# Five reorderings in a single-core two-block kernel: first unit by passes, taps, convolution, additions, weight halves

## What is computed

```python
# first block
hn = rmsnorm(h, norm1_g); proj = hn @ w_in
u, q, k, v, g_ssm, g_att = split(proj)
y_ssm = s5_mixer(u, ...)            # diagonal complex state space, scanned, then a gated unit
o = diff_attention(q, k, v, ...)    # 4 heads, two softmaxes each, causal, ALiBi
mixed = sigmoid(g_ssm) * (y_ssm @ w_ssm_out) + sigmoid(g_att) * (y_att @ w_att_out)
h = h + mixed @ w_o
h = h + conv_glu_ffn(rmsnorm(h, norm2_g), w_up, conv_w, conv_b, w_down)
# second block
z = rms_norm(x, norm_mix) @ w_in
a_x, a_y, b_q, b_f, b_i, b_g, c_q, c_k, c_v = split(z)
ya = rglru_group(a_x, a_y, ...)     # convolution of 4 taps, gates, a scan
yb = hgrn2_group(b_q, b_f, b_i, b_g, ...)
yc = moba_group(c_q, c_k, c_v)      # 8 heads, causal
x = x + concat(rms_norm(ya), yb, rms_norm(yc)) @ w_out
x = x + square(relu(rms_norm(x, norm_mlp) @ w_ff1)) @ w_ff2
out = rms_norm(x, norm_final)
```

## Time and profile before

| | |
|---|---|
| median of 3 runs | 721.42 us (719.54 to 721.86) |
| the profiled execution's own time | 720.89 us |
| its span, first to last instruction | 719.2 us |
| TensorE busy | 702.1 us, 98% of the span |
| VectorE, ScalarE, GpSimd busy | 75%, 54%, 4% |
| mean granted TensorE clock | 0.996 |
| chain that ended last, by engine | PE 80%, DVE 13%, ACT 4%, issue 3% |

### The profile page before, as it was taken

How to read it: one execution, slowest core, us unless ns; L and a number is a source line. 1 busy time by engine, 2 the same in 40 slices (tenths; PEclk the granted TensorE clock), 3 DMA queues, 4 the chain that set the end, 5 groups by cost and what they waited for, 6 DMA issues and landing times.

```text
span 719.2 us, 14645 instructions
## 1 busy us (share of the span) xinstructions
PE 702.1 (98%) x6172; PEld 664.1 (92%) x6172; DVE 536.1 (75%) x953; ACT 390.4 (54%) x600; POOL 26.0 (4%) x50
## 2 busy tenths in 40 slices
PE   7999998999999999999999999999999999999997
PEld 6999997888999999999999989889999899998995
DVE  6899899557978877777678899965877655655653
ACT  7586557368366454444445874498653444434433
POOL 3001000000000000000000340000000000000000
PEclk9999999999999999999999999999999999999999
DMA  8752343233555555555555553333355556655541
GB/s 248 218 167 61 95 147 112 62 111 125 179 173 180 195 193 194 177 176 181 189 198 193 186 167 127 118 118 118 118 190 185 182 176 193 200 191 177 187 165 59
DMA packets 94701, 115.68 MB, mean 161 GB/s; under 512 B 7971, under 2 KB 83932, under 8 KB 94636
## 3 DMA queue, kind: packets, MB, share of 16 engines
q1 hardware_dynamic: 94244, 114.51, 48.8%
q0 software_dynamic: 128, 0.13, 0.1%
q10 hardware_dynamic: 264, 0.10, 0.1%
HBM read 113.69 MB, written 1.05 MB: 160 GB/s over the span
## 4 chain that ended last, share of the span: by engine, by line
PE 80%; DVE 13%; ACT 4%; issue 3%; POOL 0%; DVEq 0%; POOLq 0%; ACTq 0%
PE psum L1842 16%; PE psum L1843 16%; PE psum L1844 16%; PE psum L2440 4%; PE psum L2438 4%; PE psum L2439 4%; DVE w_lo L1101 3%; PE psum L2196 3%; PE psum L2200 3%; PE psum L2198 3%; ACT w_hi L500 1%; PE psum L1989 1%; PE psum L2024 1%; PE psum L1934 1%; DVE sz L1020 1%
## 5 line engine op out<-in xcount | busy, mean ns | idle before, releaser
L1101 DVE TENSOR_TENSOR w_lo<-w_raw,w_hi 128x2048 fp32r<-128x2048 f32 x105 | 239.4, 2289 | 70.1 <-ACT w_hi L500 69.9
L500 ACT ACTIVATE w_hi<-w_raw 128x2048 fp32r<-128x2048 f32 x105 | 199.0, 1906 | 57.2 <-PE psum L2440 28.2
L1842 PE MATMUL psum<-x2n_hi,w_hi 128*128 128x256 f32 x400 | 114.3, 286 | 1.7 <-DVE w_lo L1101 0.7
L1843 PE MATMUL psum<-x2n_lo,w_hi 128*128 128x256 f32 x400 | 112.0, 280 | 0.0
L1844 PE MATMUL psum<-x2n_hi,w_lo 128*128 128x256 f32 x400 | 112.0, 280 | 0.0
L1842 PE MATMUL psum<-hs_hi,w_hi 128*128 128x256 f32 (+1 forms) x352 | 99.6, 283 | 0.0
L1843 PE MATMUL psum<-hs_lo,w_hi 128*128 128x256 f32 (+1 forms) x352 | 99.2, 282 | 0.0
L1844 PE MATMUL psum<-hs_hi,w_lo 128*128 128x256 f32 (+1 forms) x352 | 98.9, 281 | 0.0
L1842 PEld LDWEIGHTS psum<-x2n_hi,w_hi 128*128 128x128 f32 x400 | 75.2, 188 | 4.9 <-DVE x2n_lo L1562 1.0
L1844 PEld LDWEIGHTS psum<-x2n_hi,w_lo 128*128 128x128 f32 x400 | 76.2, 191 | 0.0
L1843 PEld LDWEIGHTS psum<-x2n_lo,w_hi 128*128 128x128 f32 x400 | 75.2, 188 | 0.6
(11 more groups left out here) (461 smaller groups left out, 1535.0 us busy)
## 6 DMA issues: line engine op xcount, KB each, us to landing
w_raw<-in_w_ff_dram SPq DMA_DIRECT2D x32, 1024.0 KB, 5.2
w_raw<-in_w_in_dram SPq DMA_DIRECT2D x27, 1024.0 KB, 5.3
w_raw<-in_w_up_dram SPq DMA_DIRECT2D x22, 1024.0 KB, 5.1
w_raw<-in_w_down_dram SPq DMA_DIRECT2D x11, 1024.0 KB, 5.0
w_raw<-in_w_o_dram SPq DMA_DIRECT2D x4, 1024.0 KB, 5.1
w_raw<-in_w_out_dram SPq DMA_DIRECT2D x4, 1024.0 KB, 5.4
w_raw<-in_w_ssm_out_dram SPq DMA_DIRECT2D x2, 1024.0 KB, 5.1
w_raw<-in_w_att_out_dram SPq DMA_DIRECT2D x2, 1024.0 KB, 5.1
```

What stands on the lines that cost most here:

```text
L500: A.activation(w_hi[:, u % NW, :], raw[:, u % NRAW, :], ACT.Copy).then_inc(sem("hi_ready"), 1)
L1101: V.tensor_tensor(w_lo[:, u % NRAW, :], raw[:, u % NRAW, :], w_hi[:, u % NW, :].bitcast(F32), ALU.subtract).then_inc(sem("lo_ready"), 1)
L1842: T.matmul(out_, lh, rh, start=start, stop=False)
L1843: T.matmul(out_, lh, rl, start=False, stop=False)
```

## The change

In the first unit the loops over passes and groups change places: each pass is done for both groups before the next. On ScalarE `split_to(14)` and the tanh of gate unit 3 move behind the output's copy, the exponentials and the taps' copies; on VectorE `split_to(14)` moves behind the second half's scan, mix and back-rotation. In the second block one `scale` of `hgq` moves ahead of the small columns, `lru_conv(1)` moves behind level 5 and `m_norm(1)`, and `m_max(1)` ahead of a weight half. At the output unit the scaling of `mo` comes ahead of `hgg`, all four of its low halves behind the reciprocal, and each weight half behind both of a unit's additions instead of between the first addition and its low half. Nothing is added or removed; the numbers of instructions of each kind stay the same.

```diff
--- before.py
+++ after.py
@@ -719,12 +719,12 @@
             copy_b(0)
             outputs_by_phase()
             gates(2)
-            split_to(14)
-            gates(3)
             copy_o(0)
             exp_b(1)
             copy_a(1)
             taps()
+            gates(3)
+            split_to(14)
             split_to(15)
             exp_a(2)
             gates(4)
@@ -1671,6 +1671,7 @@
             for m in range(2):
                 scale("hg_f", 0, m, hgf[:, m, :])
             two_after("hg_f")
+            scale("hg_q", 0, 0, hgq[:, 0, :])
             dve.wait_ge(sem("tiny_a"), 3)
             seq(V.tensor_scalar(sm("sp_m", 2), lam, -1.0, 0.0, ALU.mult, ALU.max))
             seq(tt(sm("sp_m", 2), sm("sp_m", 2), sm("sp_l", 2), ALU.add))
@@ -1685,8 +1686,7 @@
                 seq(V.tensor_scalar(hgf[:, m, :], hgf[:, m, :], sm("lb_c", 2)[:, m:m + 1], sm("lb_m", 2)[:, m:m + 1],
                                     ALU.mult, ALU.add))
                 seq(V.tensor_scalar(hgk[:, m, :], hgk[:, m, :], sm("lb_c", 2)[:, m:m + 1], None, ALU.mult))
-            for m in range(2):
-                scale("hg_q", 0, m, hgq[:, m, :])
+            scale("hg_q", 0, 1, hgq[:, 1, :])
             two_after("hg_q")
             dve.wait_ge(sem("w2_act"), 6)
             tt(hqf[:, :, :], hgq[:, :, :], hgf[:, :, :], ALU.mult).then_inc(sem("h_level"), 1)
@@ -1706,15 +1706,15 @@
             scale("lru_x", 0, 1, lru_g[:, 1, :])
             level(3)
             two_after("lru_x")
-            lru_conv(1)
             scale("cq", 1, 0, cq[:, 2, :], 0.125)
             level(4)
             scale("cq", 1, 1, cq[:, 3, :], 0.125)
+            m_max(1)
             two_after("cq", 1)
-            m_max(1)
             scale("ck", 1, 0, ck[:, 2, :])
             level(5)
             m_norm(1)
+            lru_conv(1)
             two_after("ck", 1)
             scale("ck", 1, 1, ck[:, 3, :])
             level(6)
@@ -1750,7 +1750,6 @@
             V.reciprocal(sm("hg_root", 8), sm("hg_root", 8)).then_inc(sem("hg_r"), 1)
             dve.wait_ge(sem("yc_rms"), 1)
             seq(V.reciprocal(rst3[:, :], rst3[:, :]))
-            scale("hg_g", 0, 0, hgg[:, 0, :])
 
             def y_low(n_, kt, src):
                 dve.wait_ge(sem("ycat_hi"), n_ + 1)
@@ -1759,11 +1758,10 @@
             for p_ in range(4):
                 STT(out=mo[:, p_, :], in0=mo[:, p_, :], scalar=col("att_norm", p_), in1=rst3[:, :],
                     op0=ALU.mult, op1=ALU.mult).then_inc(sem("yc"), 1)
-            for p_ in range(2):
-                y_low(p_, 4 + p_, mo[:, p_, :])
+            scale("hg_g", 0, 0, hgg[:, 0, :])
             dve.wait_ge(sem("ya_rms"), 1)
             mark(V.reciprocal(rst2[:, :], rst2[:, :]))
-            for p_ in range(2, 4):
+            for p_ in range(4):
                 y_low(p_, 4 + p_, mo[:, p_, :])
             dve.wait_ge(sem("dve_seq"), n[0])
             for m in range(2):
@@ -1794,10 +1792,9 @@
                     tt(x2[:, 2 * i + m, :], x2[:, 2 * i + m, :], banks[g % NB][:, 0:256], ALU.add).then_inc(
                         sem(f"group_free{g % NB}"), 1)
                     x3_square(2 * i + m - 1)
-                    if m == 0:
-                        split_to(unit_at[("w_out2", i)]["n"] + 3 - i // 3)
                     taken(dve, g)
                     x_low("x3", "norm_mlp", 2 * i + m)
+                split_to(unit_at[("w_out2", i)]["n"] + 3 - i // 3)
             x3_square(7)
             split_to(unit_at[("ff1", 0)]["n"] + 2)
             dve.wait_ge(sem("norm_root"), 2)
@@ -1924,8 +1921,8 @@
             def first_unit():
                 wh, wl = (w[:, 0, :].rearrange("p (k n) -> p k n", k=KD) for w in (w_hi, w_lo))
                 for h in range(2):
-                    for m in range(2):
-                        for n_, (w, x) in enumerate(((wh, xn_hi), (wh, xn_lo), (wl, xn_hi))):
+                    for n_, (w, x) in enumerate(((wh, xn_hi), (wh, xn_lo), (wl, xn_hi))):
+                        for m in range(2):
                             if m == 0 and n_ != 1:
                                 pe.wait_ge(sem((("first_hi", "hi_ready")[h], "", ("first_lo", "lo_ready")[h])[n_]), 1)
                             for kt in range(4 * h, 4 * h + 4):
@@ -1933,8 +1930,8 @@
                                     pe.wait_ge(sem(("xn_hi", "xn_lo")[n_]), kt + 1)
                                 last = T.matmul(banks[m][:, 0:TOK], w[:, kt, P * m:P * m + P], x[:, kt, :],
                                                 start=(kt == 0 and n_ == 0), stop=(kt == KD - 1 and n_ == 2))
-                        if h == 1:
-                            last.then_inc(sem("group_done"), 1)
+                            if h == 1 and n_ == 2:
+                                last.then_inc(sem("group_done"), 1)
 
             def second_unit():
                 wh, wl = w_hi[:, 1, :].rearrange("p (k n) -> p k n", k=KD), w_lo[:, 1, :].rearrange("p (k n) -> p k n", k=KD)
```

## The result

The changed kernel takes 713.63 us (median of six executions, 711.83 to 715.46); the kernel before took 720.48 us beside it (six, 717.79 to 721.86). The profiled execution of the changed kernel took 714.82 us (span 713.1) against 720.89 (span 719.2).

A forecast was written before the change was run, and what follows sets the result against it. TensorE is busy nearly throughout; seven rows of its waits hold 7.0 us. Terms 1.0 + 2.4 + 0.0 + 1.0 + 0.6 + 0.8 = 5.8 us off 720.89 give 715.1, forecast as 715.5 us, range 713.9 to 718.4.

The forecast's parts named there:

- Rival 3: Whole kernel: the gain is a loan, transfers or a full engine set the pace; 719.3 to 721.4 us, chance 9%.
- First unit: Group 1's 8 matmuls run ahead of the wait for w_lo; 1.0 us won if the slow clock stretch stays.
- The ceiling: First unit's gain at unit 3 is at most 1.7 us, since VectorE's w_lo ends at 31.67 us at the earliest.
- Rival 1: The clock holds in the first unit: 0.7 us more won there, 714.8 us, chance 20%.
- Rival 5: Alternating PSUM banks in the first unit loses the clock: 3 us lost, 718.5 us, chance 2%.
- Taps: Attention output's copy on ScalarE starts at 115.05 instead of 117.45 us, ahead of a weight half: 2.4 us won.
- hgq: Scaling ahead of the small columns removes a 0.4 us wait, which moves on to hqf: 0.0 us.
- Convolution: lru_conv(1) behind level 5 removes TensorE's 0.9 us wait for that level's copy, plus the restart: 1.0 us won.
- Output unit: mo's additions first win 0.6 us; weight halves behind both rounds win 0.8 us.
- Rival 2: A close margin of four fails: one miss gives back 0.7 us, several up to 2.5; 716.2 to 718.0 us, chance 24%.
- the other three margins: Slack of 0.3 to 0.5 us at the output unit's half, level 5's copy and m_norm(1).
- Rival 4: Output unit's halves come late if a round takes 2.6 us or more, not 1.46; at 3 us, 724.8 us; chance 3%.

The follow-up runs named there:

- e15: The kernel before, unedited, one more profiled execution: 718.33 us.
- e12: The changed kernel, unedited, run a third time: median 713.24 us, ratio to the kernel before 0.9874.
- e4: The changed kernel with the weight half and gate unit 3's tanh back ahead of the attention output's copy: 718.94 us.
- e2: The changed kernel with the scaling of hgq back behind the small columns: 714.81 us.
- e5: The changed kernel with lru_conv(1) and m_max(1) back where they stood before: 714.07 us.
- e6: The changed kernel with hgg's scaling ahead of the output unit's four additions again and the low halves in two pairs: 715.47 us.
- e7: The changed kernel with each weight half of the output unit back between the first addition and its low half: 715.32 us.
- e1: The changed kernel, unedited, run again: median 714.74 us, ratio to the kernel before 0.9904.
- e16: The changed kernel with the first unit's order of before, one more profiled execution: 717.41 us.
- e13: The kernel before, unedited, one more profiled execution: 720.55 us.
- e3: The changed kernel with the first unit's groups one after the other again: 715.18 us.
- e9: The changed kernel, but TensorE's level-0 scores no longer wait for the product hqf: 714.74 us.
- e10: The changed kernel with level 0's copy hA ahead of a weight half and the second scaling of cq: 712.40 us.
- e11: The changed kernel with the edits of e9 and e10 together: 713.99 us, ratio to the kernel before 0.9873.
- e14: The kernel before, unedited, one more profiled execution: 721.50 us.

## Why the prediction was right, and where it was wrong

**What bounds it.** Right in the main: the gain lies at the places of the waits, and no transfer or engine took it back. Their sum fell by 4.4 us (7.0 to 2.6) and the span by 6.1, since in the first unit work also runs at another clock. Rival 3 (a loan) is out: from the mark 547 to the last matmul all 18 profiles take 160.52 us, before and after.

**First unit.** 1.0 us taken, 1.48 between the two first profiles and 1.45 on average: under-sized, between the bounds of 1.0 and 1.7. The 1.0 us for 8 matmuls is right for the end of the unit (0.96, e15 against e12), but at unit 3 VectorE's half swallows it where the clock is up in both; what arrives there is the clock's part. The mistake was to take the slow stretch of one profile as fixed. It did not stay where it was: the upper level was granted for good from 9 to 16 us in the twelve profiles of the new order, and from 17 to 19 us in five of the six with the old (11 us in e15). The ceiling held: I had VectorE's `w_lo` at 31.67 us at the earliest, and no profile has unit 3 before 31.73.

**Rival 1** (the clock holds) has happened in some executions, e12 among them, with unit 3 at 31.73 us, 1.6 us sooner than before, where I had 1.7. That the clock holds is not the new order's doing alone: it held in e15 too. **Rival 5** (alternation costs) is out: in e12 the 8-matmul rows in the new order step by 0.126 us, in e15's old order by 0.125. The section of the Trainium skill on cycling through PSUM banks ("TensorE: Matmul & The Clock Gate", "A second HAM failure mode: psum-queue depth-cycling") does not describe this unit; the measurement decides.

**Taps.** 2.4 us taken, 2.36 between the first profiles and 2.40 in e4. Right; what I did not see is that a wait this long can also cost the clock, 1.5 us in e15. Four of the five profiles with this wait kept the clock there.

**`hgq`.** 0.0 taken; 0.35 us lost between the first profiles, 0.1 to 0.25 against e2. The mechanism is right (the wait moved to `hqf`, 1.1 us where I had about 0.7), but the remainder is a loss and not nothing.

**Convolution** 1.0 taken, 1.01 and 0.99 (e5). **Output unit**, 0.6 + 0.8 taken: 0.60 (e6), and for the halves 1.06 between the first profiles, 0.70 in e7. **Rival 2** did not come true: the half at unit 3 did wait, 0.27 us, but as a part of the ceiling above, and the other three margins held. **Rival 4** is out: a round still takes 521.68 - 520.22 = 1.46 us in the changed kernel:

```profile
520.22 0.42 DVE L1020 TENSOR_TENSOR x<-x,psum 128x256 f32<-128x256 f32 x1
...
521.68 0.41 DVE L1020 TENSOR_TENSOR x<-x,psum 128x256 f32<-128x256 f32 x1
```

**The sum.** By the table 1.48 + 2.36 - 0.35 + 1.01 + 0.60 + 1.06 = 6.2 us against the 5.8 that I had; the profiled execution came out at 714.82 us, where I had it at 715.1. Up to here the prediction holds to 0.3 us, though by luck in part: the first unit gave 0.5 us more than I had, and `hgq` took 0.35 back.

**The step that failed** is the last one, from the profiled execution to the median: "the median of the runs shown is 0.5 us above that execution, so I say 715.5", with a low end of 713.9. It took an execution to be one number with a small error. It is one of two numbers 3.1 us apart. Both profiled executions had the longer one (134.98 us between 260 and 395), and three of the six executions behind the median lie in the lower group, so had the shorter by all that the profiles show: 711.83, 712.22, 712.44. The median of six fell between the groups, below the range. The upper group alone has its middle at 715.1 us, inside the range. With the largest first-unit gain the prediction's sum is 714.8 us; for the 0.9 us from there to the low end it names no term, and a draw of the matmuls' step, 3.1 us, was not in it. The three times of before that I had (719.54 to 721.86) already spread by 2.3 us, and I took no account of that. That this is the size of the matter, the later runs show: e1 and e12, the same program, have medians of 714.74 and 713.24 us.

Apart from that, the gain itself is larger than the pair of profiles tells: 51 executions of the kernel before, from the times of e1 to e16, have a median of 721.34 us and the 19 of the changed kernel 713.84, 7.5 us apart. Of the 51, 43 have a mean clock of 0.996 or less; of the 19, none is below 0.998. The clock is seen to fall in three of the four profiles of the kernel before: in the first unit, from 13.7 to 17.1 us, in the first profile and in e13, and at the taps in e15. In no profile of another kernel does it fall before the last microseconds. Eight of e4's twelve executions have a mean of 0.996 or less and none of the nine of e3 and e16, so the falls come with the order at the taps; why it can also fall in the first unit of the kernel before is left open. e4's groups lie 3.0 and 4.1 us above the changed kernel's where its marks have 2.4, so 0.6 to 1.7 us are the size of it, enough for the 1.3 us between 6.2 and 7.5. How much of these is the clock and how much the draw of the step, no run shows: one profile for each kernel shows too few executions.

## What to carry to other kernels

Before turning a sum into a median and a range, look at the spread of the single times: if it is larger than the terms, the range must hold it, and a gain is then read from the starts of the same instruction in two traces, stretch by stretch, not from medians of six. A wait of two or three us on TensorE can cost more than its length, since the clock may be taken away behind it (1.5 us here, e15); price it with both, and compare two orders of work at a like clock, as e15 and e12, before a gain is put down to the order. And where a wait has only moved one step on, look at what stands in the late engine's queue ahead of both steps: each of two edits alone gave next to nothing (e9, e10), the pair gave 1.1 to 1.2 us (e11).

## What the hardware showed that I had not expected

Matmuls of 128x256 that follow each other without a wait, at a granted clock of 1.00 throughout, step by 113 ns in some executions and by 118 ns in others of the same program. The view of groups has them at 281 and 276 ns each; first the changed kernel, then e1, 262 to 394 us:

```profile
L2193 PE MATMUL psum<-ff_hi,w_hi 128*128 128x256 f32 x116 | 32.6, 281 | 0.0
```
```profile
L2193 PE MATMUL psum<-ff_hi,w_hi 128*128 128x256 f32 x125 | 34.5, 276 | 0.0
```

From mark 260 to 395 a pattern of 144 matmuls repeats: some 96 of them step by 117.8 or by 113.3 ns, the other 48 by 120 ns in either case, so the stretch takes 3.1 us less and not 5. Elsewhere in the program it also takes two values: between the marks 510 and 530, 19.71 us in some profiles and 20.45 in e5, e9, e10 and e11, with no wait more (0.3 us for `w_lo` in these as in the others). e14, of the kernel before, has the longer step there too, and its stretch is no longer (20.54 us): what the step costs is saved at the wait for `x2n_lo` behind it, 0.5 us in e15's view of waits and not listed in e14's. I found nothing that decides it (not the clock, not the start of the stretch, not the edits); that is left open.
